# Three of ten turned probability slabs copied by VectorE in the grouped attention heads of a transformer layer

## The reference

```python
def attend(q, k, v, scale):
    ...
    def one_block(qi):
        sc = jnp.einsum("bqhgd,bkhd->bhgqk", qi, k, preferred_element_type=jnp.float32) * scale
        p = jax.nn.softmax(sc, axis=-1).astype(v.dtype)
        return jnp.einsum("bhgqk,bkhe->bqhge", p, v)

def mix_groups(dq, dk, dv, gq, gk, gv, lam, lam_init, subln_g):
    ...
    o1 = attend(dq[:, :, :, 0], dk[:, :, :, 0], dv, sc)
    o2 = attend(dq[:, :, :, 1], dk[:, :, :, 1], dv, sc)
    o_diff = rmsnorm(o1 - lam.astype(o2.dtype) * o2, subln_g) * (1.0 - lam_init)
    o_gqa = attend(gq, gk, gv, sc)
```

## Time and profile before

| what | value |
|---|---|
| time, median of 3 executions (lowest to highest) | 2238.73 us (2238.4 to 2242.18) |
| time of the profiled execution | 2243.67 us |
| its span in the trace | 2242.0 us |
| busy: PE, DVE, ACT, POOL | 1991.6, 1559.7, 1388.4, 964.8 us |
| attention, grouped units 4 to 11 in the trace | about 527.8 to 681.5 us |
| attention, grouped units 16 to 23 in the trace | about 791.4 to 927.5 us |
| distance from one grouped unit to the next | 17.91 us (oT_head copied at 563.74, 581.65, 599.55 us) |

### The profile page before, as it was taken

The page is one execution under the profiler, slowest core; times in us unless marked ns, Lnnn a source line. Parts: engine busy times, 40 slices in busy tenths (PEclk is TensorE's granted clock), DMA queues, the critical chain, the costliest instruction groups (busy, mean ns, idle before and its releaser), DMA issues.

```text
span 2242.0 us, 36447 instructions
## 1 busy us (share of the span) xinstructions
PE 1991.6 (89%) x9610; PEld 1488.2 (66%) x9610; DVE 1559.7 (70%) x2176; ACT 1388.4 (62%) x2012; POOL 964.8 (43%) x875
## 2 busy tenths in 40 slices
PE   4899994788889899779989999999999999999990
PEld 2676663555556555566637888888877888888880
DVE  3752472684336643355537999999988999999995
ACT  2421121565666566423327998889978998889991
POOL 1010111661125510025553666666655666666664
PEclk8999997899999999889999999999999999999995
DMA  7464345711122111349447999789999977789856
GB/s 258 137 186 134 105 140 184 213 29 41 36 45 44 37 39 29 134 134 143 130 108 269 302 364 307 213 272 319 360 334 349 347 237 234 210 239 365 244 147 238
DMA packets 162987, 429.17 MB, mean 191 GB/s; under 512 B 27329, under 2 KB 82369, under 8 KB 138225
## 3 DMA queue, kind: packets, MB, share of 16 engines
q1 hardware_dynamic: 92802, 294.36, 36.6%
q0 software_dynamic: 60400, 116.90, 23.4%
q10 hardware_dynamic: 9712, 16.99, 2.6%
HBM read 361.95 MB, written 96.26 MB: 204 GB/s over the span
## 4 chain that ended last, share of the span: by engine, by line
PE 39%; DMA 7%; DVE 4%; issue 3%; ACT 2%; ACTq 1%; SPq 1%; DVEq 1%; POOL 0%; POOLq 0%
PE ps_d L1961 9%; PE ps_r L1946 7%; PE ps_r L1948 6%; PE ps_r L1947 6%; DMA w_experts<-in_w_exp_down 5%; PE ps_y L1869 4%; PE ps_y L1936 3%; ACT w_gate_up_high L1513 1%; PE ps_g L1886 1%; PE ps_d L1903 1%; ACTq L1254 1%; DMA y_scratch<-e_y,e_target_index 1%; DVE w_gate_up_low L1726 1%; DMA y_scratch<-y_shared 1%; PE ps_g L1968 1%
## 5 line engine op out<-in xcount | busy, mean ns | idle before, releaser
L1726 DVE TENSOR_TENSOR w_gate_up_low<-w_experts,w_gate_up_high 128x1024 fp32r<-128x1024 f32 x424 | 498.6, 1217 | 21.2 <-ACT w_gate_up_high L1513 21.1
L1513 ACT ACTIVATE w_gate_up_high<-w_experts 128x1024 fp32r x424 | 425.0, 1050 | 29.3 <-SPq L1280 14.5
L940 DVE TENSOR_REDUCE neg_max<-ps_scores 128x1 f32<-128x1280 f32 x128 | 190.3, 1490 | 234.6 <-PE ps_scores L1025 234.2
L1946 PE MATMUL ps_r<-w_gate_up_high,gatheredT_high 128*128 128x512 f32 x840 | 339.0, 404 | 5.3 <-DVE gatheredT_low L1732 5.3
L1948 PE MATMUL ps_r<-w_gate_up_high,gatheredT_low 128*128 128x512 f32 x840 | 330.1, 393 | 0.0
L1947 PE MATMUL ps_r<-w_gate_up_low,gatheredT_high 128*128 128x512 f32 x840 | 328.2, 391 | 0.0
L1405 POOL DMA_INDIRECT y_scratch<-e_y,e_target_index x104 | 272.7, 2622 | 103.4 <-POOL e_target_index L1401 94.2
L1755 DVE TENSOR_TENSOR w_down_low<-w_experts,w_down_high 128x2048 fp32r<-128x2048 f32 x104 | 238.4, 2292 | 50.4 <-ACT w_down_high L1532 49.8
L1392 POOL DMA_INDIRECT gathered<-h_scratch,e_gather_index x108 | 201.4, 1864 | 97.5 <-POOL e_gather_index L1389 91.5
L1532 ACT ACTIVATE w_down_high<-w_experts 128x2048 fp32r x104 | 199.9, 1922 | 40.0 <-issue 40.0
L1025 PE MATMUL ps_scores<-k_high_low,q_high 128*128 128x512 f32 (+1 forms) x384 | 167.7, 437 | 57.0 <-DMA k_high_low<-k_scratch 29.4
(11 more groups left out here) (256 smaller groups left out, 3954.6 us busy)
## 6 DMA issues: line engine op xcount, KB each, us to landing
w_experts<-in_w_exp_gate SPq DMA_DIRECT2D x64, 1024.0 KB, 9.5
w_experts<-in_w_exp_up SPq DMA_DIRECT2D x64, 1024.0 KB, 12.8
w_experts<-in_w_exp_down SPq DMA_DIRECT2D x64, 1024.0 KB, 17.7
w_mod_later<-in_w_mod ACTq DMA_DIRECT2D x32, 512.0 KB, 3.7
w_mod_first<-in_w_mod SPq DMA_DIRECT2D x4, 2048.0 KB, 15.6
w_in_raw<-in_w_in SPq DMA_DIRECT2D x32, 256.0 KB, 3.6
k_high_low<-k_scratch POOLq DMA_DIRECT2D x10, 640.0 KB, 8.6
values<-in_tokens SPq DMA_DIRECT2D x10, 512.0 KB, 11.3
```

The lines of the kernel that those rows point to most:

```text
L1513: act.activation(split_slice(eH, j), raw_slice(ring, slot, j), ACT.Copy).then_inc(X["wH"], 1)
L1726: nc.vector.tensor_tensor(split_slice(eL, j), raw_slice(ring, slot, j), split_slice(eH, j).bitcast(F32), ALU.subtract).then_inc(X["wL"], 1)
L1946: nc.tensor.matmul(psR[:], xH[:, k], eH[:, k], start=(k == 0), stop=False)
```

## The change

VectorE gets an `out_p` of its own. In grouped units it copies slabs 1, 5 and 8 from PSUM to SBUF and counts them on a new semaphore, `s_evd`; ScalarE skips these three and copies the other seven. Differential units are as before. TensorE waits for the semaphore of the engine that made the copy, and a product over two slabs waits for both.

```diff
+    def by_dve(g):
+        return units[g // KT_N][0] == "g" and g % KT_N in (1, 5, 8)
+
+    def wait_out(eng, g):
+        if by_dve(g):
+            eng.wait_ge(s_evd, sum(1 for h in range(g + 1) if by_dve(h)))
+        else:
+            eng.wait_ge(s_ev, sum(1 for h in range(g + 1) if not by_dve(h)))
...
             def out_p(u, kt):
                 g = u * KT_N + kt
+                if by_dve(g):
+                    return
                 act.wait_ge(s_tr, g + 1)
...
+            def out_p(u, kt):
+                g = u * KT_N + kt
+                if not by_dve(g):
+                    return
+                dve.wait_ge(s_tr, g + 1)
+                if g >= KEEP:
+                    dve.wait_ge(s_pv, g - KEEP + 1)
+                nc.vector.tensor_copy(pd[:, g % KEEP], pT(u, kt)).then_inc(s_evd, 1)
...
                 for kt in range(KT_N):
+                    out_p(u, kt)
                     if kt in at:
                         rowmax(u + 1, at[kt])
...
                 if g is not None:
-                    pe.wait_ge(s_ev, g + 1)
+                    wait_out(pe, g)
...
-                pe.wait_ge(s_ev, g + 1)
+                if kind == "g":
+                    wait_out(pe, g - 1)
+                wait_out(pe, g)
```

More of the change, by code:

```diff
@@ L776, in attention @@
         s_ev = b.sem(ph, "probsT_out")
+        s_evd = b.sem(ph, "probsT_out_dve")
         s_pv = b.sem(ph, "pv_done")
```

## The result

The changed kernel takes 2228.35 us (median of 5 executions, 2224.0 to 2230.42), the kernel before in the same runs 2242.18 us (5, 2238.4 to 2244.0). The ratio is 0.9936, 95% interval 0.9923 to 0.9949, so the gain lies between 0.51 and 0.77%, some 11 to 17 us. The forecast was 14.5 us or 0.65% less.

A forecast was written before the change was run, and what follows sets the result against it. TensorE was taken to set the pace, so only its idle time could be won. 10.45 + 2.7 (units 4 and 16) + 1.9 + 0.5 - 1.05 = 14.5 us, from 2238.73 to 2224.2 us; range 2219.2 to 2231.

The forecast's parts named there:

- its wait at slab 3: TensorE, held by slab 1's copy behind an exponential, gains 0.95 us in each of 11 grouped units, 10.45 us.
- rival 1: The wait only moves: the exponential chain sets the period; 4 us gained, 2234.7 us; chance 0.06.
- rival 2: VectorE's queue becomes the bound: slower once a copy takes about 2 us, 2276 us at 3.30 us each; chance 0.02.
- the walk: Step-by-step timing of VectorE's order in a grouped unit: 0.34 us to spare at slab 1, 1.47 at slab 8.
- The premise that GpSimd computes during no grouped unit except 11: Ground for expecting short VectorE copies; only unit 11's slab 5 might wait for GpSimd, losing 2.4 rather than 1.05 us.
- Unit 10: Single bank, every copy on the path: slab 2 gains 0.4 us, slab 6 0.73, slab 9 0.80, together 1.9.
- Unit 11: VectorE's copy of slab 5 stands behind the row maximum of row 4: 1.05 us lost.
- Unit 22: Its last product waits for slab 9's copy, earlier once slab 8 leaves ScalarE: 0.48 us, besides 0.95 at slab 3.
- Busy time: Over the kernel, VectorE busy 33 us more and ScalarE 29 us less.
- A further semaphore shows no cost: 48 TensorE products wait for one more semaphore: no cost expected, at most 0.05 us each or 2.4 us in all.
- rival 3: Every longer VectorE copy is on the path: 48 x (0.684 - 0.60) = 4.0 us lost, 2242.7 us; chance 0.01.
- The stage behind: Stage after the attention, granted clock 0.83: starting 14 us earlier may shift its clock stretches, 3 us either way.

The follow-up runs named there:

- the eighth experiment: Kernel before, all copies on ScalarE, with the exponential of row 1 behind slab 1's copy (grouped units with a grouped successor): ratio to before 0.9932.
- the second experiment: Changed kernel, but VectorE copies only slabs 5 and 8 and slab 1 stays on ScalarE: ratio to the kernel before 0.9988.
- the third experiment: Changed kernel, but VectorE copies slabs 3, 6 and 9 in place of 1, 5 and 8: ratio to the kernel before 1.0001.
- the fourth experiment: Changed kernel, but slab 5 of unit 11 back on ScalarE: ratio to the kernel before 0.9909.

## Why the prediction was right

The mechanism was the one that the prediction names, and the unit lengths test it term by term, as below. The total tests it less: the interval of the ratio is 6 us wide, and in the two profiled executions unit 12 gave 1.1 us and everything outside units 4 to 23 took 0.7 us more, neither of which the sum contains. That these nearly cancel is luck. The time itself came out 4.1 us above the forecast 2224.2, mostly since the kernel before now measured 2242.18 us, 3.5 above the base that was used.

- *TensorE sets the pace and its wait at slab 3 is worth 0.95 us.* Right: 0.97 to 0.98 in each of ten units, and ScalarE's order alone gives the same (the eighth experiment). It was read by comparing the spacing of transposes that don't wait with that of those that do; the 0.77 us in the bracket alone would have given 2 us too little over 11 units.
- *The wait for the exponential moves along and doesn't take the gain back* (rival 1). Right, by the rows of 576.28 to 579.28.
- *VectorE's order has room* (rival 2). Right: copies of 0.69 us, free room of 0.27 us at slab 1 and 1.63 at slab 8 where the walk had 0.34 and 1.47. The premise that GpSimd computes during no grouped unit except 11 was not quite right: the trace of before has a small operation of it early in units 4 and 16 (L857, 1.02 us); in the trace of after no copy ran beside either of them.
- *Unit 10.* 1.89 against 1.9. By the experiments slab 1's copy gives 0.37 of it and those of slabs 5 and 8 1.52. *Unit 11.* 1.07 lost against 1.05, by the named cause; putting the copy back restores it. Of the bounds for it, 1.05 and 2.4, the short one held: the copy took 0.68 us in the middle of GpSimd's 2.89 us.
- *Unit 22.* 1.39 against 1.43; slab 1's 0.90 and, by the second experiment, 0.40 for slabs 5 and 8.
- *Busy time.* VectorE's rose by 30.9 us (1559.7 to 1590.6), near the 33 forecast. ScalarE's fell by 24.7 (1388.4 to 1363.7) and not by 29: copies in a row overlap in the rows (two of 0.60 us take 1.09), so taking one away frees less than its length. The gain didn't depend on it.
- *A further semaphore shows no cost.* Right as far as the rows go: a product that now waits for three (the first of each unit) starts 0.53 us after the start of the transposes ahead of it, as in the earlier trace rows:

```profile
567.62 0.60 PE L1061 MATMUL ps_scores<-ident,probs 128*128 128x128 f32 x4
...
568.15 1.08 PE L1079 MATMUL ps_out<-probsT,values 128*64 128x512 f32 x4
```

- *The longer VectorE copy counts* (rival 3). It does not. The copy is longer, 0.69 against 0.60 us, and it cost nothing. The Trainium skill ("Perfetto Trace Analysis", Optimizing Scalar/DVE Operations) gives VectorE more overhead on PSUM than ScalarE, about 125 against 51 ns. The trace agrees on that order, with 0.09 us between the two copies. Yet in the third experiment, where the three copies were not the late ones, handing them to VectorE brought nothing: it is the place of a copy that counts.
- *The stage behind* had a granted clock of 0.85 in its window instead of 0.83, and all stages behind the attention together were 1.8 us shorter, within the 3 us allowed.

What the prediction did not see: in ten units the same gain of 0.98 us was to be had on ScalarE alone, by the place of one exponential.

## What to carry to other kernels

When an engine waits for a short operation, look first at what stands in front of that operation in its own engine's order, and try to move that; another engine is the second choice, and it brings its own order with it (unit 11). The worth of a wait is the difference to the spacing without one, and the room that an added operation has is read from when its successor is wanted: here the first came out to 0.03 us and the second to 0.16. An edit that moves an exponential later in its unit is worth more once nothing short stands behind that exponential (0.55 us per unit alone, 0.90 after the other edit), so orders that share an operation are to be tried together.

## What was new of the hardware

**An operation from PSUM ran beside GpSimd undisturbed where one with two SBUF inputs did not.** In unit 11 VectorE's copy out of PSUM took 0.68 us while GpSimd's two-input operation was running. The reciprocal behind it (L959, one input, in SBUF) kept its 0.15 us as well. The next VectorE operation with two SBUF inputs, L960, took 0.48 instead of 0.22 us and ended with GpSimd's (663.96 + 0.48 = 664.44 against 661.53 + 2.89 = 664.42). The product of two SBUF tiles in `finish_norm` (L1000) varied from 0.69 to 3.30 us; the longest ones started inside a GpSimd operation (one at 462.66 us, GpSimd's from 462.03 to 465.41) and ended 0.55 us behind it. The copies out of PSUM (L974) hardly varied at all (min/median/max in ns):

```profile
L1000 DVE TENSOR_TENSOR o_tile<-o_head,sub_gain x8: 691/1996/3302, 462.7 to 792.0; 128x512 f32<-128x512 f32 x8
L974 DVE COPY probsT<-ps_scores x48: 678/692/693, 531.4 to 908.2; 128x512 f32<-128x512 f32 x48
```

The Trainium skill describes this ("SBUF — State Buffer", Summary: rules for kernel authors): when a VectorE operation has two SBUF inputs and GpSimd's reads SBUF, the second to issue waits until the first is done. The trace agrees, with the times above.

**Unit 12 varied from 26.2 to 28.4 us without any edit in it.** It is 28.38 us before, 27.25 after, 26.20 in the fourth experiment. Windows of its length give the granted clock (columns as in rows 1), of the kernel before:

```profile
682.82:711.20 28.38, 26.70 (x117) 18.66 (x117) 16.64 (x21) 17.36 (x27) 15.32 (x8) 0.88 0.21 42
```

and of the kernel after:

```profile
678.26:705.50 27.24, 25.54 (x117) 17.86 (x117) 17.12 (x21) 17.36 (x27) 15.32 (x8) 0.94 0.21 44
```

0.88 and 0.94 are means of stretches at 2.4 and at 1.2 GHz. By windows of half a microsecond the stretch at 1.2 lasted some 6.8 us before (from about 685.5) and 3.4 after (from about 680.7). The other traces fall in line: in seven of them the mean clock of unit 12 was 1.00 and the unit took 26.20 to 26.23 us, in three it was 0.94 and the unit took 27.37 to 27.51. So the length of unit 12 follows the granted clock. Why it is granted 1.2 GHz there in some executions and not in others is not settled here. The waiting for a late slab 5 in unit 11 does not decide it: in the second experiment unit 11 was as long as in the kernel after (26.41 us), and the clock in unit 12 stayed at 1.00:

```profile
682.70:708.91 26.21, 23.79 (x115) 16.74 (x116) 17.12 (x21) 17.34 (x29) 15.30 (x8) 1.00 0.23 45
```
